# State steps of a gated delta rule: one product for two, smaller fill parts, another order on VectorE

## The chip, the cores and the metric

The kernel runs on one core of a Trainium2 chip. The metric is the device time of one execution in microseconds (us). The kernel is written instruction by instruction for each engine (TensorE or PE, VectorE or DVE, ScalarE or ACT, GpSimd or POOL, and SP, which issues the loads); the engines are kept in order by semaphores alone.

## The reference

Two layers of a decoder over 256 tokens of width 2048, all in float32:

```python
for l in range(DEPTH):                          # 2
    h = rms_norm(x, norm_mix_pre[l])
    p = h @ w_in[l]                             # columns shared out among three mixers
    mix = concat[gated_deltanet(6 heads), multiscale_pool(4 groups), swa_attention(6 heads)] @ w_out[l]
    x = x + rms_norm(mix, norm_mix_post[l])
    x = x + rms_norm(conv_glu_ffn(rms_norm(x, norm_ffn_pre[l])), norm_ffn_post[l])
```

The change lies in the delta rule. The 256 tokens are four chunks of 64 (C=64), a head is 128 wide, and after products within the chunks (an inverse, u, w, a_intra) a state S of 128x128 per head is carried over the chunks:

```python
def step(S, xs):
    u_n, w_n, q_n, k_n, a_n, c_n = xs
    v_new = u_n - w_n @ S
    o_n = q_n @ S + a_n @ v_new
    S = S * c_n + k_n.T @ v_new
    return S, o_n
```

Here q_n is q decayed within its chunk, and a_n is the attention within the chunk. The output o then goes through an RMS norm over the head and is multiplied by silu(z).

## The kernel before

**Large products.** A product with a weight matrix is made in fp32r as three: the weights are split into a high part (`w_hi`, ScalarE, L942) and the rest (`w_lo`, VectorE, L1159), so are the activations (`h_hi`, `h_lo`), and hi*hi, hi*lo and lo*hi are added up in PSUM (`three`, L1507). Weights come in pairs of column tiles, 2 MB each, into `raw` (two slots), issued by SP (L805), which waits until the `w_lo` parts of the pair two before are made. A pair has four parts of 1024 columns (four rows of k tiles), `hi_part` and `lo_part` make them, and TensorE uses a part in two halves (`half_a`, L1557), twelve records of 256 columns each; for `w_out` it is `out_half` (L1695), six records of 512 columns.

**Groups.** In the mixing stage the delta rule runs over three groups (NG) of two heads. TensorE's program for a group is `delta_pe` (L668). Wherever it would wait for VectorE or ScalarE it has fill: `more(count)` does the next `count` halves of the projection that later groups need (32 halves in each group). How many stand where is written out by hand in `FILL_FULL` (the first two groups, a loop) and `FILL_LAST` (the last group, whose fill is the pool projection's last part and the beginning of the output projection). VectorE's program is `delta_dve` (L493), ScalarE's `delta_act` (L362). Theirs have `more(place)` too: there it makes the low and high part number `place`, which TensorE uses some parts later.

**A state step.** A matrix of four [128,128] blocks m = 2h+t holds head h and token tile t; chunk c is half of such a tile. The four steps n have t = n // 2, c = n % 2. In a step TensorE waits for `state_ready`, makes w@S for both heads into bank 2 (L730), then q@S into bank 6 (L736), does one half of fill, waits for `v_new_ready`, makes the state's addition (L743) and adds a@v_new to bank 6 (L749). The stationary side of w and q has 64 columns, so these products are tiles of 128*64. VectorE makes v_new (L577) after w@S, and after L743 updates the state of both heads (L590), drains and releases the next step. Between these VectorE has a `w_lo` part (`more(11)`, after the first v_new) and the taps of the causal convolution for the next group's values (`taps`, L1391: three taps, two tiles each, every tap waits for the one before): taps 1 and 2 after the second v_new, tap 3 after the third. The convolution is begun by ScalarE (L1065).

**After the steps.** ScalarE squares o (L404) and copies it (L405), VectorE sums and scales it, GpSimd takes the root, VectorE normalizes (L604), TensorE turns it into bank 7, and VectorE multiplies by silu(z) (L608), which releases `delta_out`. Meanwhile TensorE does fill and turns the next group's q, k and v into banks 2 to 4 (or, in the last group, does the pool product, `pool_pe`).

An fp32 product is two records in the trace (two passes), an fp32r product one.

Of the kernel before, what the change touches and what calls it, by code (L numbers as in the profile page):

```python
# [98 lines left out]
                 states=(1, 1, 1, 1), out=2, end=0)  # L99
FILL_LAST = dict(turned=7, normed=2, products=2, n_turned=1, residual=(1, 1, 1, 1, 1), step=(1, 1, 1, 1, 1), uw=2,  # L100
                 states=(1, 1, 1, 1), out=2, end=2)
# [42 lines left out]
def trunk(nc, a, out):  # L144
    with ExitStack() as ctx:
# [60 lines left out]
        (q_s, k_s, v_s, z_s, qn, qd, kn, kbeg, kdec, vb, kn_t, qn_t, qd_t, e1, e2, vs, gb) = (  # L206
            scr[:, i, :] for i in range(17))
        pw, resid, inv, attn, u_m, w_t, o_m, low_m = q_s, k_s, v_s, qn, qd, kn, e1, e1
        v_new, state = vs[:, 0:256], vs[:, 256:512]

# [136 lines left out]
        def pool_act(act, l):  # L347
            act.wait_ge(sem("pool_mixed"), l + 1)
            for g in range(NPOOL):
                ins = act.activation(act_t[:, T_POOL + g, :], ps[:, 2 + g // 2, (g % 2) * T:(g % 2 + 1) * T],  # L350
                                     ACT.Copy, scale=par_all[:, l, R_PS + g:R_PS + g + 1])
# [10 lines left out]
        def delta_act(act, l, g, more, begin, ahead, last=False):  # L362
# [130 lines left out]
        def delta_dve(dve, l, g, more, finish, taps, windowed=lambda: None, second=3):  # L493
            v = l * NG + g + 1
            dve.drain()
# [77 lines left out]
            for n in range(4):  # L573
# [4 lines left out]
                                  ps[r, 2, 0:256].rearrange("p (h n) -> p h n", h=2),  # L578
                                  ALU.subtract).then_inc(sem("v_new_ready"), 1)
                if n == 0:  # L580
                    more(11)
                if n == 1:
                    taps(2, (1, 2))
                if n == 2:
                    taps(2, (3,))
                if n < 3:
                    dve.wait_ge(sem("state_add"), 3 * v - 2 + n)
                    for h in range(2):
                        sh = state[:, h * P:(h + 1) * P]
                        dve.scalar_tensor_tensor(sh, sh, gate_g[:, 5 + c, 2 * h + t:2 * h + t + 1],  # L590
                                                 ps[:, 3, h * P:(h + 1) * P], ALU.mult, ALU.add)
# [1264 lines left out]
```

## Time and profile before

| | us |
|---|---|
| median of 3 runs | 2325.9 |
| lowest and highest | 2325.8 and 2326.24 |
| the profiled execution | 2326.02 |
| its span, first to last instruction | 2324.2 |
| TensorE busy in it | 2305.2 (99%) |
| VectorE busy | 1617.7 (70%) |
| ScalarE busy | 1073.8 (46%) |

The granted clock of TensorE was 0.999 of its full speed. Busy time counts records, and those of TensorE overlap one another, since a product streams in while the one before drains; so a busy TensorE is not one at its peak, and what a piece of work costs on it is read from the starts of the records.

### The profile page before, as it was taken

How to read it: one execution, taken by the hardware profiler on the slowest of the kernel's cores; microseconds unless marked ns; L12 is line 12 of the kernel's file. 1: busy time of each engine (PE TensorE's matmuls, PEld its weight loads, DVE VectorE, ACT ScalarE, POOL GpSimd, SP SyncE). 2: the span in 40 equal slices, each digit the busy share in tenths (PEclk: the TensorE clock that was granted, in tenths of full speed). 3: DMA queues.
4: the chain of work that ended last, by engine and by line, in shares of the span. 5: the costliest groups of instructions: out<-in, count | busy, mean ns of one | idle time of the engine just before them, and what ended most of it. 6: DMA issues, size and time to landing. Idle time of an engine off the chain costs nothing.

```text
span 2324.2 us, 37134 instructions
## 1 busy us (share of the span) xinstructions
PE 2305.2 (99%) x13964; PEld 2041.7 (88%) x13964; DVE 1617.7 (70%) x2287; ACT 1073.8 (46%) x1398; POOL 39.5 (2%) x55
## 2 busy tenths in 40 slices
PE   9999999999999999999999999999999999999998
PEld 9999988888888888888899999888888888888887
DVE  5876665877787778555568676658778787785455
ACT  5454434644444444444455444346444444444443
POOL 0000010000000000000000000100000000000000
PEclk9999999999999999999999999999999999999999
DMA  7533326555665556555544433275655565555553
GB/s 243 170 121 109 124 94 204 177 180 183 196 195 185 180 187 215 194 182 203 199 146 146 137 102 124 74 235 168 193 181 180 193 195 190 180 201 207 188 185 141
DMA packets 295368, 401.29 MB, mean 173 GB/s; under 512 B 9320, under 2 KB 269570, under 8 KB 283522
## 3 DMA queue, kind: packets, MB, share of 16 engines
q1 hardware_dynamic: 294996, 400.19, 52.2%
q8 instruction: 49, 0.80, 0.1%
q10 hardware_dynamic: 302, 0.12, 0.0%
q14 instruction: 21, 0.17, 0.0%
HBM read 398.20 MB, written 2.10 MB: 172 GB/s over the span
## 4 chain that ended last, share of the span: by engine, by line
PE 94%; DVE 3%; DVEq 1%; ACT 1%; issue 1%; DMA 0%; ACTq 0%; SPq 0%; POOLq 0%; POOL 0%
PE ps L1528 28%; PE ps L1509 15%; PE ps L1510 15%; PE ps L1511 15%; PE ps L1534 14%; PE ps L673 2%; PE ps L678 1%; PE ps L730 1%; DVE w_lo L1159 1%; PE ps L743 1%; DVEq L1387 0%; ACT w_hi L942 0%; PE ps L736 0%; PE ps L1657 0%; DMA raw<-in_w_in 0%
## 5 line engine op out<-in xcount | busy, mean ns | idle before, releaser
L942 ACT ACTIVATE w_hi<-raw 128x1024 fp32r<-128x1024 f32 x740 | 779.7, 1059 | 984.1 <-PE ps L1534 522.1
L1159 DVE TENSOR_TENSOR w_lo<-raw,w_hi 128x1024 fp32r<-128x1024 f32 x744 | 895.8, 1224 | 465.4 <-ACT w_hi L942 457.5
L1528 PE MATMUL ps<-h_both,w_hi 128*128 128x512 f32 x2816 | 885.3, 396 | 1.2 <-DVE h_both L1181 1.2
L1534 PEld LDWEIGHTS ps<-h_both,w_lo 128*128 128x128 f32 x2816 | 529.0, 188 | 124.7
L1534 PE MATMUL ps<-h_both,w_lo 128*128 128x256 f32 x2816 | 553.9, 278 | 0.0
L1528 PEld LDWEIGHTS ps<-h_both,w_hi 128*128 128x128 f32 x2816 | 428.9, 189 | 1.9 <-issue 1.6
L1509 PE MATMUL ps<-w_hi,h_both 128*128 128x512 f32 x960 | 376.1, 392 | 0.9 <-DVE w_lo L1159 0.9
L1511 PE MATMUL ps<-w_hi,h_both 128*128 128x512 f32 x960 | 373.7, 389 | 0.0
L1510 PE MATMUL ps<-w_lo,h_both 128*128 128x512 f32 x960 | 373.7, 389 | 0.0
L1509 PE MATMUL ps<-h_both,w_hi 128*128 128x256 f32 x1216 | 354.7, 292 | 2.1 <-DVE h_both L1181 2.1
L1510 PE MATMUL ps<-h_both,w_hi 128*128 128x256 f32 x1216 | 343.8, 283 | 0.0
L1511 PE MATMUL ps<-h_both,w_lo 128*128 128x256 f32 x1216 | 343.7, 283 | 0.0
L1509 PEld LDWEIGHTS ps<-h_both,w_hi 128*128 128x128 f32 x1216 | 232.8, 191 | 6.0 <-issue 5.9
L1510 PEld LDWEIGHTS ps<-h_both,w_hi 128*128 128x128 f32 x1216 | 232.9, 192 | 0.1
L1511 PEld LDWEIGHTS ps<-h_both,w_lo 128*128 128x128 f32 x1216 | 232.6, 191 | 0.0
L1509 PEld LDWEIGHTS ps<-w_hi,h_both 128*128 128x128 f32 x960 | 180.2, 188 | 39.6 <-issue 2.9
L1511 PEld LDWEIGHTS ps<-w_hi,h_both 128*128 128x128 f32 x960 | 180.2, 188 | 37.7
L1510 PEld LDWEIGHTS ps<-w_lo,h_both 128*128 128x128 f32 x960 | 180.3, 188 | 36.4
L1471 DVE SCALAR_TENSOR_TENSOR scratch<-scratch,par 128x255 f32<-128x255 f32 (+1 forms) x352 | 154.6, 480 | 29.5 <-issue 28.9
L673 PE MATMUL ps<-scratch 128*128 128x128 f32 x672 | 86.9, 275 | 0.6 <-DVE scratch L555 0.6
L673 PEld LDWEIGHTS ps<-scratch 128*128 128x128 f32 x672 | 81.8, 191 | 2.5 <-DVE scratch L555 1.5
L1464 DVE TENSOR_SCALAR scratch<-scratch,par 128x256 f32<-128x256 f32 x176 | 64.7, 410 | 18.4 <-issue 18.1
(201 smaller groups left out, 1251.6 us busy)
## 6 DMA issues: line engine op xcount, KB each, us to landing
raw<-in_ffn_w_up SPq DMA_DIRECT2D x88, 2048.0 KB, 8.0
raw<-in_ffn_w_down SPq DMA_DIRECT2D x44, 2048.0 KB, 7.7
raw<-in_w_in SPq DMA_DIRECT2D x37, 2048.0 KB, 8.2
raw<-in_w_out SPq DMA_DIRECT2D x64, 512.0 KB, 6.4
x<-in_x SPq DMA_DIRECT2D x4, 512.0 KB, 7.0
raw<-in_w_in SPq DMA_DIRECT2D x4, 512.0 KB, 8.6
scratch<-in_norm_mix_post SPq DMA_DIRECT2D x2, 1024.0 KB, 9.5
scratch<-in_norm_ffn_post SPq DMA_DIRECT2D x2, 1024.0 KB, 10.0
```

The lines of the kernel that those rows point to most:

```text
L673: ins = pe.matmul(ps[:, bank, m * P:(m + 1) * P], w[:, m, :], r[:, m, :], start=True, stop=True)
L678: ins = pe.transpose(ps[:, bank, m * P:(m + 1) * P], mats(src)[:, m, :], ident)
L730: ins = pe.matmul(ps[r, 2, h * P:(h + 1) * P], w_t[:, cols], state[:, h * P:(h + 1) * P], start=True, stop=True)
L942: act.activation(w_hi[:, own(q, s), :], raw_part(l, q, s), ACT.Copy).then_inc(hi_done, 1)
L1159: dve.tensor_tensor(w_lo[:, own(q, s), :], raw_part(l, q, s), w_hi[:, own(q, s), :].bitcast(F32), ALU.subtract).then_inc(lo_done, 1)
L1464: dve.tensor_scalar(y_ab[:, ab, i, :], summed[:, ab, i, :], par_all[:, l, bass.ds(2 * j + (R_FC + 2 * 2 * FT + ab * FT + i), 1)], par_all[ ...
L1471: ins = dve.scalar_tensor_tensor(y, summed[:, ab, i, 0:T - k], par_all[:, l, bass.ds(2 * j + (R_FC + (2 - k) * 2 * FT + ab * FT + i), 1)], ...
L1509: pe.matmul(dst, w, xs, start=start, stop=False, skip_group_check=True)
L1510: pe.matmul(dst, w, xl, start=False, stop=False, skip_group_check=True)
L1511: return pe.matmul(dst, wl, xs, start=False, stop=True, skip_group_check=True)
L1528: pe.matmul(ps[:, up_bank(q - P_UP, i), :], w_hi[:, own(q, s), c:c + P], h_both[:, k, :, :].rearrange("p a n -> p (a n)"), start=k == 0, s ...
L1534: return pe.matmul(ps[:, up_bank(q - P_UP, i), 0:T], w_lo[:, own(q, s), c:c + P], h_hi[:, k, :], start=False, stop=True, skip_group_check= ...
```

## The change

Four edits in the state steps:

1. **Joint stationary side.** w and the decayed q are laid side by side in one buffer `wq` (for each block and chunk 64 columns of w beside 64 of q), and one product with 128 stationary columns gives w@S in one half of the rows of a bank and q@S in the other. For chunk 0 the bank is 6 with w in rows 0 to 63, for chunk 1 it is bank 2 with w in rows 64 to 127. The attention product adds to the half that holds q@S. The output so lies in two banks, by chunk, with its row halves exchanged, and is copied and squared in two pieces; the product with silu(z) undoes the exchange.
2. **Quarters.** Fill is done in quarters (one k tile of a part, six records of 256 columns, or one output tile, three of 512). A step has one quarter in the wait for v_new and one more after the attention product (`steps`); what is left over goes to `out`.
3. **Update by heads.** Each head's addition has a bank of its own (3 and 7) and a semaphore increment of its own, and TensorE waits for each head's state by itself.
4. **Taps.** In the groups that aren't last, tap 1 follows the first v_new, tap 2 the first update, tap 3 the second v_new; the `w_lo` part of place 11 follows the fourth v_new, and places 12 and 13 move back by one point each.

Before it turns the next group's q, k and v (or does the pool product, now in banks 3 and 6), TensorE waits for the output's copies.

```diff
-                 states=(1, 1, 1, 1), out=2, end=0)
+                 states=(0.5, 0.5, 0.5, 0.5), steps=(0.5, 0.5, 0.5), out=2.5, end=0)
...
+        wq = scr[:, 5:7, :].rearrange("p a (m n) -> p (a m) n", m=2).rearrange("p m (c n) -> p m c n", c=4)
+        w_of, qd_of = wq[:, :, 0:4:3, :], wq[:, :, 1:3, :]
+
+        def state_bank(c):
+            return 2 if c else 6
...
-            for i, dst in enumerate((kn_t, qn_t, qd_t)):
+            for i, dst in enumerate((kn_t, qn_t)):
                 act.wait_ge(sem("normed_turned"), 3 * v - 2 + i)
                 act.activation(dst, ps[:, 5 + i, :], ACT.Copy).then_inc(sem("normed_copied"), 1)
+            act.wait_ge(sem("normed_turned"), 3 * v)
+            act.activation(qd_of, ps[:, 7, :].rearrange("p (m c n) -> p m c n", m=4, c=2),
+                           ACT.Copy).then_inc(sem("normed_copied"), 1)
...
-            act.wait_ge(sem("o_done"), v)
-            act.activation(e2, ps[:, 6, :], ACT.Square).then_inc(sem("o_squared"), 1)
-            act.activation(o_m, ps[:, 6, :], ACT.Copy).then_inc(sem("o_copied"), 1)
+            for c in range(2):
+                act.wait_ge(sem("o_done"), 2 * v - 1 + c)
+                r = slice(CH * (1 - c), CH * (2 - c))
+                act.activation(e2[r, :], ps[r, state_bank(c), :], ACT.Square).then_inc(sem("o_squared"), 1)
+                act.activation(o_m[r, :], ps[r, state_bank(c), :], ACT.Copy).then_inc(sem("o_copied"), 1)
...
-            dve.tensor_copy(w_t, ps[:, 7, :])
+            dve.tensor_copy(w_of, ps[:, 7, :].rearrange("p (m c n) -> p m c n", m=4, c=2))
...
                 dve.tensor_tensor(v_new[r, :].rearrange("p (h n) -> p h n", h=2), mats(u_m)[r, t::2, :],
-                                  ps[r, 2, 0:256].rearrange("p (h n) -> p h n", h=2),
+                                  mats(ps[r, state_bank(c), :])[:, t::2, :],
                                   ALU.subtract).then_inc(sem("v_new_ready"), 1)
-                if n == 0:
+                if last and n == 0:
                     more(11)
-                if n == 1:
-                    taps(2, (1, 2))
-                if n == 2:
-                    taps(2, (3,))
+                if not last and n < 2:
+                    taps(2, (1 + 2 * n,))
+                if not last and n == 3:
+                    more(11)
                 if n < 3:
-                    dve.wait_ge(sem("state_add"), 3 * v - 2 + n)
                     for h in range(2):
+                        dve.wait_ge(sem("state_add"), 6 * v - 5 + 2 * n + h)
                         sh = state[:, h * P:(h + 1) * P]
                         dve.scalar_tensor_tensor(sh, sh, gate_g[:, 5 + c, 2 * h + t:2 * h + t + 1],
-                                                 ps[:, 3, h * P:(h + 1) * P], ALU.mult, ALU.add)
-                    dve.drain().then_inc(sem("state_ready"), 1)
+                                                 ps[:, 3 + 4 * h, 0:P], ALU.mult,
+                                                 ALU.add).then_inc(sem("state_ready"), 1)
+                    dve.drain()
+                    if not last and n == 0:
+                        taps(2, (2,))
...
-            more(13)
+            more(13 if last else 12)
...
-            more(14, 15)
+            more(*((14, 15) if last else (13, 14, 15)))
...
-                pe.wait_ge(sem("state_ready"), 4 * v - 3 + n)
                 for h in range(2):
                     m = 2 * h + t
-                    cols = slice(m * P + CH * c, m * P + CH * (c + 1))
-                    ins = pe.matmul(ps[r, 2, h * P:(h + 1) * P], w_t[:, cols], state[:, h * P:(h + 1) * P],
-                                    start=True, stop=True)
+                    pe.wait_ge(sem("state_ready"), 8 * v - 7 + 2 * n + h)
+                    ins = pe.matmul(ps[:, state_bank(c), m * P:(m + 1) * P],
+                                    wq[:, m, 2 * c:2 * c + 2, :].rearrange("p c n -> p (c n)"),
+                                    state[:, h * P:(h + 1) * P], start=h == 0, stop=False, skip_group_check=True)
                 ins.then_inc(sem("ws_done"), 1)
-                for h in range(2):
-                    m = 2 * h + t
-                    cols = slice(m * P + CH * c, m * P + CH * (c + 1))
-                    pe.matmul(ps[r, 6, m * P:(m + 1) * P], qd_t[:, cols], state[:, h * P:(h + 1) * P],
-                              start=h == 0, stop=False, skip_group_check=True)
                 more(fill["states"][n])
                 hold(pe, sem("v_new_ready"), 4 * v - 3 + n)
                 if n < 3:
                     for h in range(2):
                         m = 2 * h + t
-                        ins = pe.matmul(ps[:, 3, h * P:(h + 1) * P], kdec[r, m * P:(m + 1) * P],
-                                        v_new[r, h * P:(h + 1) * P], start=True, stop=True)
-                    ins.then_inc(sem("state_add"), 1)
+                        pe.matmul(ps[:, 3 + 4 * h, 0:P], kdec[r, m * P:(m + 1) * P], v_new[r, h * P:(h + 1) * P],
+                                  start=True, stop=True).then_inc(sem("state_add"), 1)
                 for h in range(2):
...
-                    ins = pe.matmul(ps[r, 6, m * P:(m + 1) * P], attn[r, cols], v_new[r, h * P:(h + 1) * P],
-                                    start=False, stop=True, skip_group_check=True)
-                if n == 3:
+                    ins = pe.matmul(ps[CH * (1 - c):CH * (2 - c), state_bank(c), m * P:(m + 1) * P], attn[r, cols],
+                                    v_new[r, h * P:(h + 1) * P], start=False, stop=True, skip_group_check=True)
+                if n >= 2:
                     ins.then_inc(sem("o_done"), 1)
+                if n < 3:
+                    more(fill["steps"][n])
             more(fill["out"])
+            pe.wait_ge(sem("o_copied"), 2 * v)
...
-            def half_a(l, q, j, n, s, half):
-                if half == 0:
+            def quarter_a(l, q, j, n, s, kk):
+                if kk == 0:
...
-                for kk in (2 * half, 2 * half + 1):
-                    ins = both_tiles(q, s, kk)
-                if half == 1:
+                ins = both_tiles(q, s, kk)
+                if kk == 3:
                     ins.then_inc(sub_used, 1)
```

## Rows read from the trace of the kernel before

**Rows 1.** The page: engines' busy time, and the chain that ended last.
```profile
PE 2305.2 (99%) x13964; PEld 2041.7 (88%) x13964; DVE 1617.7 (70%) x2287; ACT 1073.8 (46%) x1398; POOL 39.5 (2%) x55
...
PE 94%; DVE 3%; DVEq 1%; ACT 1%; issue 1%; DMA 0%; ACTq 0%; SPq 0%; POOLq 0%; POOL 0%
```
**Rows 2.** Timeline, TensorE, 194.3 to 200.4: start, duration, engine, line, operation, out<-in.
```profile
195.17 0.65 PE L730 MATMUL ps<-scratch 128*64 128x128 f32 x4 [0.15 <-DVEq L592]
...
196.18 0.39 PE L1509 MATMUL ps<-h_both,w_hi 128*128 128x256 f32 x1
196.41 0.28 PE L1510 MATMUL ps<-h_both,w_hi 128*128 128x256 f32 x1
...
197.59 0.28 PE L1511 MATMUL ps<-h_both,w_lo 128*128 128x256 f32 x1
197.80 0.71 PE L743 MATMUL ps<-scratch 64*128 64x128 f32 x4
198.44 0.65 PE L749 MATMUL ps<-scratch 64*64 64x128 f32 x4
199.24 0.65 PE L730 MATMUL ps<-scratch 128*64 128x128 f32 x4
```
**Rows 3.** Timeline, TensorE, last group of the first layer.
```profile
343.39 0.65 PE L730 MATMUL ps<-scratch 128*64 128x128 f32 x4
...
347.43 0.65 PE L730 MATMUL ps<-scratch 128*64 128x128 f32 x4
```
**Rows 4.** Timeline, TensorE, 186.2 to 188.3: the inverse's last products.
```profile
186.22 0.28 PE L1511 MATMUL ps<-h_both,w_lo 128*128 128x256 f32 x1
...
186.33 1.95 PE L673 MATMUL ps<-scratch 128*128 128x128 f32 x16
...
188.04 0.36 PE L1509 MATMUL ps<-h_both,w_hi 128*128 128x256 f32 x1
...
188.24 0.28 PE L1510 MATMUL ps<-h_both,w_hi 128*128 128x256 f32 x1
```
**Rows 5.** Timeline, TensorE, entry to the first step and exit of the fourth.
```profile
190.87 0.28 PE L1511 MATMUL ps<-h_both,w_lo 128*128 128x256 f32 x1
...
191.08 0.65 PE L730 MATMUL ps<-scratch 128*64 128x128 f32 x4
...
205.95 0.65 PE L749 MATMUL ps<-scratch 64*64 64x128 f32 x4
...
206.53 0.39 PE L1509 MATMUL ps<-h_both,w_hi 128*128 128x256 f32 x1
...
209.51 1.91 PE L678 MATMUL ps<-const,scratch 128*128 128x128 f32 x16
```
**Rows 6.** Timeline of VectorE and ScalarE; one line's durations; the page's w_lo row.
```profile
191.77 0.41 DVE L577 TENSOR_TENSOR scratch<-scratch,ps 64x256 f32<-64x256 f32 x1
...
192.23 0.90 ACT L1065 ACTIVATE act_t<-scaled,par 128x256 f32 x2
...
197.40 0.88 DVE L1391 SCALAR_TENSOR_TENSOR act_t<-scaled,par,act_t 128x254 f32 x2 [0.21 <-issue]
...
198.55 0.60 DVE L590 SCALAR_TENSOR_TENSOR scratch<-scratch,gate_g,ps 128x128 f32<-128x128 f32 x2 [0.27 <-PE ps L743]
...
L590 DVE SCALAR_TENSOR_TENSOR scratch<-scratch,gate_g,ps x36: 339/344/348, 194.5 to 1501.2; 128x128 f32<-128x128 f32 x36
...
L1159 DVE TENSOR_TENSOR w_lo<-raw,w_hi 128x1024 fp32r<-128x1024 f32 x744 | 895.8, 1224 | 465.4 <-ACT w_hi L942 457.5
```
**Rows 7.** Timeline, SP; DMA issues in 185 to 230, last column landing time.
```profile
193.48 19.55 SPq L805 DMA_DIRECT2D raw<-in_w_in  x2
...
raw<-in_w_in SPq DMA_DIRECT2D x2, 2048.0 KB, 8.1
```
**Rows 8.** Timeline, start of the second group.
```profile
216.15 2.12 ACT L942 ACTIVATE w_hi<-raw 128x1024 fp32r<-128x1024 f32 x2
...
222.77 1.47 PE L678 MATMUL ps<-const,scratch 128*128 128x128 f32 x12
```

More of the change, by code:

```diff
@@ L98 @@
 FILL_FULL = dict(turned=8, normed=2, products=2, n_turned=1, residual=(1, 1, 1, 1, 1), step=(1, 1, 1, 1, 2), uw=2,
-                 states=(1, 1, 1, 1), out=2, end=0)
+                 states=(0.5, 0.5, 0.5, 0.5), steps=(0.5, 0.5, 0.5), out=2.5, end=0)
 FILL_LAST = dict(turned=7, normed=2, products=2, n_turned=1, residual=(1, 1, 1, 1, 1), step=(1, 1, 1, 1, 1), uw=2,
-                 states=(1, 1, 1, 1), out=2, end=2)
+                 states=(0.5, 0.5, 0.5, 0.5), steps=(0.5, 0.5, 0.5), out=2.5, end=2)
 FEW_LATER = {0: 0, 1: 1, 3: 2, 4: 3, 5: 4, 7: 5, 8: 6, 9: 7, 10: 8, 11: 9, 12: 10, 14: 11, 15: 12}
@@ L491, in swa_dve, with delta_dve @@
             finish(1)
-        def delta_dve(dve, l, g, more, finish, taps, windowed=lambda: None, second=3):
+        def delta_dve(dve, l, g, more, finish, taps, windowed=None, second=3):
             v = l * NG + g + 1
+            last = windowed is not None
             dve.drain()
@@ L565, in delta_dve @@
             dve.wait_ge(sem("uw_done"), v)
-            dve.tensor_copy(w_t, ps[:, 7, :])
+            dve.tensor_copy(w_of, ps[:, 7, :].rearrange("p (m c n) -> p m c n", m=4, c=2))
             dve.memset(state, 0.0)
-            dve.drain().then_inc(sem("state_ready"), 1)
+            dve.drain().then_inc(sem("state_ready"), 2)
             finish(2)
@@ L1520, in part_a @@
                 if q < P_UP:
-                    for half in range(2):
-                        half_a(l, q, j, n, s, half)
+                    for kk in range(4):
+                        quarter_a(l, q, j, n, s, kk)
                 else:
@@ L1693, in out_tile, with out_quarter @@
                              w_hi[:, s, cols], w_lo[:, s, cols], xp == 0 and k == 0)
-            def out_half(l, u, k):
+            def out_quarter(l, u, k, t):
                 q, s, kind, xp = out_sub(u)
-                if k == 0:
+                if k == 0 and t == 0:
                     if u == 0:
@@ L1702, in out_half @@
                     pe.wait_ge(lo_done, l * SUBS + (4 * q + s + 9))
-                for t in range(TT):
-                    ins = out_tile(l, u, t, k, int(kind[1]), k)
-                if k == 1:
+                ins = out_tile(l, u, t, k, int(kind[1]), k)
+                if k == 1 and t == 1:
                     ins.then_inc(sub_used, 1)
@@ L1713, in out_rest @@
                         for k in range(2):
-                            out_half(l, u, k)
+                            for t in range(TT):
+                                out_quarter(l, u, k, t)
                         continue
@@ L1794, in more_of @@
                 def more_of(q, j, halves):
-                    left = iter(range(halves))
+                    left = iter(range(2 * halves))
                     def more(count):
-                        for n in itertools.islice(left, count):
-                            half_a(l, q + n // 8, j, q + n // 8, n // 2 % 4, n % 2)
+                        for n in itertools.islice(left, int(2 * count)):
+                            quarter_a(l, q + n // 16, j, q + n // 16, n // 4 % 4, n % 4)
                     return more
@@ L1807, in more_last @@
                 def more_last():
-                    left = iter(range(16 + 2 * N_SOON))
+                    left = iter(range(32 + 4 * N_SOON))
                     def more(count):
-                        for n in itertools.islice(left, count):
-                            if n < 16:
-                                half_a(l, P_POOL + n // 8, 0, P_POOL + n // 8, n // 2 % 4, n % 2)
+                        for n in itertools.islice(left, int(2 * count)):
+                            if n < 32:
+                                quarter_a(l, P_POOL + n // 16, 0, P_POOL + n // 16, n // 4 % 4, n % 4)
                             else:
-                                out_half(l, (n - 16) // 2, n % 2)
+                                out_quarter(l, (n - 32) // 4, n // 2 % 2, n % 2)
                     return more
```

25 lines of the change are left out of this document (14 added, 11 removed).

## The prediction

> **What bounds the kernel now.** I read the page first. TensorE is busy for 99% of the span and carries 94% of the chain that ended last, VectorE 3% [rows 1]. A change pays only if it takes time out of TensorE's own stream: fewer passes, cheaper switches between kinds of work, or less idling at its waits. VectorE, ScalarE and the loads matter only where they come late for it.
>
> Then I read TensorE's timeline through the state steps (two layers, three groups, four steps: 24 steps), since only they change what TensorE computes. In these rows an fp32 product is two records ("x4" is two products) and durations overlap, so I work with differences of starts. One cycle of the middle steps [rows 2]: the w product starts at 195.17, the q product follows, the fill (twelve fp32r records, a half part) at 196.18, the state product at 197.80, the attention product at 198.44, the next w product at 199.24. That is 4.07 us: 1.01 for w and q, 1.62 for the fill, 0.64 and 0.80 for the last two. The last 0.80 holds four passes, some 0.43, so 0.37 is idle until VectorE's update and drain are through. In the last group, whose fill has 512 columns, the cycle is 4.04 [rows 3].
>
> **Prices from the rows.** Fill records start 0.12 apart (196.41 to 197.59, ten steps) [rows 2]. Around a product of full 128*128 tiles the switch is cheap: last fill to first pass 0.11, sixteen passes in 1.71, so 0.107 each, and the first fill record then takes 0.20 to the next, 0.08 extra [rows 4]. Around half tiles (128*64, 64*128, 64*64) it is dearer: fill to w product 0.21 at 190.87 [rows 5], fill to state product 0.21, state to attention 0.64 for four passes, w and q 1.01 for eight, first fill record 0.23 [rows 2]; attention to fill 0.58 [rows 5].
>
> **The joint product (w and q in one stationary side).** Eight passes of 128*64 become four of 128*128. The trace has no such product between fills but for the inverse's, which is the same form and type, so I take its prices: 0.43 for four passes, no gap ahead, 0.20 for the first fill record. From w product to fill it is 0.43 instead of 1.01. It could cost up to twice that if loading 128 columns were what sets a pass (another 0.43 per step); the 0.107 per pass at 128 columns [rows 4] against 0.126 at 64 (1.01 over eight) speaks against it. The page "TensorE: Matmul & The Clock Gate" of the Trainium skill, section on LDWEIGHTS, says that a weight load takes time by its columns and not by its rows; by that rule four loads of 128 columns cost as much as eight of 64, and the joint product would save nothing. The trace disagrees: passes with 128 columns stand no further apart than those with 64, so the load is hidden here.
>
> **The quarter parts in both waits.** Fill work is only moved: six records ahead of the v_new wait instead of twelve, six between attention and the next w product. The second visit replaces the 0.37 of idling but brings a switch from a 64*64 tile to the fill, which the idle time now covers. Cycle after: joint product 0.43; six fill records 0.20+4x0.12+0.21=0.89; state product to attention 0.64; attention to fill 0.58; six fill records 0.23+4x0.12+0.11=0.82. Sum 3.36 against 4.07, 0.71 saved, in 18 cycles 12.8 us. In the last group a quarter is three records of 512 columns, about as long; same saving.
>
> **Ends of the chain of steps.** Ahead of the first step the gap of 0.21 becomes 0.11 or 0.12: 0.09 saved. The fourth step before: 2.63 from w to attention (as in the cycle), 0.58 to the fill, 2.98 of 24 records to the turns [rows 5]: 6.19. After: 0.43+0.89+0.58, then 30 records in 2.98+0.72: 5.60; 0.59 saved. Both six times: 4.1 us. Without stalls the change gives 12.8+4.1=16.9 us.
>
> **Does v_new arrive in time?** With less fill ahead of the wait, the margin shrinks. VectorE starts v_new 0.69 after the w product and takes 0.41 [rows 6]; with at most 0.09 to release TensorE (the update ends at 198.55+0.60, the w product starts at 199.24, a drain included [rows 2, 6]) it is ready at 1.19, the state product can start at 1.32. It is hidden by 0.13 as long as VectorE is free. The two state updates take 0.60 together, one alone 0.34 [rows 6]; by heads, the first can start some 0.5 after the state product starts, and TensorE wants the first state 2.04 after it. Hidden too, by about a microsecond.
>
> **The taps one by one.** This is where I see a cost. In the four groups that are not last, VectorE's program now has after the first v_new: tap 1 (waits until ScalarE has begun the convolution), updates, a drain, tap 2, second v_new. ScalarE's beginning ends at 192.23+0.90=193.13 [rows 6], hardly movable, as it follows the part released by the last fill ahead of the steps. The old program hid this behind a w_lo part. New: joint product at 190.99; v_new 191.7 to 192.2; tap 1 from 193.2 to 194.1 (0.88 a pair); update of head 0 until 194.45, of head 1 until 194.70. TensorE wants head 0 at 190.99+3.36=194.35 and gets it at 194.5: 0.15 lost. Then a drain (0.21, the idle time in [rows 6]) and some more for the second drain in a row, tap 2 from 195.0 to 195.9, and only then the second v_new, which could have started at 194.5+0.69=195.2: it is ready at 196.4 instead of by 195.8, 0.58 lost. The third tap follows it (0.21+0.88, to 197.5), the update ends near 198.1, TensorE wants it at 198.4: hidden. So 0.73 is lost per such group, 2.9 us in four. The last group has no taps; its w_lo part after the first v_new (1.22 [rows 6]) ends before the update is wanted.
>
> **The w_lo part moved behind the fourth v_new.** Its reader is the second quarter after the last attention product: the part is done 0.69+0.41+1.22=2.3 after the fourth joint product, wanted at 1.90+0.82=2.7: hidden by 0.4, and without that cover up to 1 us a group. SP's queue waits for this part before it issues the raw load of the pair after next. It went out at 193.48 and takes 8.1 to land [rows 7]; now, with the fourth joint product at 198.44+3.36=201.8, at about 204.2, landing at 212.3, while ScalarE first reads it near 215 (216.15 before [rows 8]; my estimate is 1 earlier now, half of what TensorE has gained by then). Hidden by 2.7; nothing is queued in SP behind it but later raw loads. The output's Square and Copy come in two row halves (twice the instructions on ScalarE, the first pair during the fourth step), TensorE's new wait for the copies before the turns has the 3.7 of 30 fill records ahead of it, the product with z in two pieces adds about 0.2 to VectorE ahead of the next group, whose turn at 222.77 [rows 8] had over 1 us to spare. The copies into strided places (w, q): same size and engine, I take no cost; if VectorE's doubled, v_new would be 0.65 late six times, 3.9 us. The attention product now goes from one row half to the other column half, the same 64*64 form: no cost taken, at most one more gap of 0.21 per step, 5.0 us.
>
> **Sum.** 16.9-2.9=14.0 us. The profiled execution took 2326.02 (span 2324.2), the median of the runs is 2325.9; so 2312.0.
>
> **Rivals.**
> - **No stall (2309).** If a tap pair and the updates overlap more than I drew, or drains in a row cost nothing, the whole 16.9 stays. Against it: ScalarE's end at 193.13 is fixed. 0.15.
> - **More waiting than drawn (2316 to 2318).** v_new's margin of 0.13 turns into a wait of 0.1 to 0.2 in all 24 steps, or the crossed tile costs its gap: 2 to 5 us less. For it: the thin margin. 0.18.
> - **The joint product costs twice (2322).** 24x0.43=10.3 us of the gain is gone, 3.7 remain, no change to be told. By the rule on weight loads this is the outcome, and the rows above speak against it. 0.04.
> - **The late raw load (slower, 2333).** If it lands later than about 12 us after its issue, ScalarE's first part of the next group, VectorE's w_lo behind it and then the normed operands are late, and TensorE stops at its turns. The gain is gone where each of the four groups loses 3.5; with 5.2 lost in each the time is 2333. In the profile the queue is otherwise empty there, so 0.03.
> - **Forecast (2310 to 2314).** 0.60.
>
> **How the numbers follow.** The likeliest is 2312. The range takes in the first two rivals and the bounds of the crossed tile and the strided copy: 2308 to 2318. A measurement of this kernel tells 0.2% (4.7 us) from no change. Forecast, no stall and more waiting are all faster: 0.93; the double price is "same", 0.04; the load is slower, 0.03.
>
> **What would show it.** In the profile after: the q product's line gone, four-record joint products of 128*128 with the fill 0.43 behind; w-product starts 3.4 apart in the last group and at the third cycle elsewhere, 3.5 and 3.9 in the first two cycles of the other groups; TensorE waiting on the second v_new there, with VectorE in tap 2; raw loads issued 10 us later with no wait on them. If cycles are 3.8 everywhere, a switch is mis-sized; if TensorE waits at v_new in the last group too, the margin was; if ScalarE waits for raw w_in, it is the load.

## The result, and the profile after

The changed kernel takes 2311.97 us (median of 4 runs, 2311.82 to 2312.16) against 2326.07 for the kernel before, measured beside it: ratio 0.9939, 95% interval 0.9922 to 0.9956. That is 14.1 us less; 14.0 was forecast (2312.0).

The page of the changed kernel, busy times and the chain that ended last:

```profile
PE 2291.5 (99%) x13868; PEld 2032.9 (88%) x13868; DVE 1618.6 (70%) x2293; ACT 1079.5 (47%) x1410; POOL 39.6 (2%) x55
...
PE 92%; DVE 3%; DVEq 1%; ACT 1%; issue 1%; DMA 0%; POOL 0%; ACTq 0%; SPq 0%; POOLq 0%
```

Against [rows 1], TensorE has 96 records fewer (13964 to 13868): the four passes of the q product in 24 steps. Its busy time falls by 13.7 us, the span by 13.8.

TensorE, VectorE, ScalarE and SP through the steps of the first group (lines have moved: the joint product is L747, the state product L756, attention L761, v_new L588, the update L601, the taps L1406, fill L1524):

```profile
191.02 0.60 PE L747 MATMUL ps<-scratch 128*128 128x128 f32 x4
...
191.38 0.37 PE L1524 MATMUL ps<-h_both,w_hi 128*128 128x256 f32 x1
...
191.66 0.41 DVE L588 TENSOR_TENSOR scratch<-scratch,ps 64x256 f32<-64x256 f32 x1
...
192.26 0.89 ACT L1080 ACTIVATE act_t<-scaled,par 128x256 f32 x2
...
192.27 0.71 PE L756 MATMUL ps<-scratch 64*128 64x128 f32 x4
...
192.91 0.65 PE L761 MATMUL ps<-scratch 64*64 64x128 f32 x4
193.42 0.88 DVE L1406 SCALAR_TENSOR_TENSOR act_t<-scaled,par,act_t 128x255 f32 x2 [1.35 <-ACT act_t L1080]
...
193.49 0.38 PE L1524 MATMUL ps<-h_both,w_hi 128*128 128x256 f32 x1
...
194.22 0.60 DVE L601 SCALAR_TENSOR_TENSOR scratch<-scratch,gate_g,ps 128x128 f32<-128x128 f32 x2
...
194.62 0.75 PE L747 MATMUL ps<-scratch 128*128 128x128 f32 x4 [0.15 <-DVE scratch L601]
...
195.11 0.88 DVE L1406 SCALAR_TENSOR_TENSOR act_t<-scaled,par,act_t 128x254 f32 x2 [0.30 <-issue]
...
196.00 0.42 DVE L588 TENSOR_TENSOR scratch<-scratch,ps 64x256 f32<-64x256 f32 x1
...
196.57 0.68 PE L756 MATMUL ps<-scratch 64*128 64x128 f32 x4 [0.50 <-DVE scratch L588]
...
198.58 0.60 PE L747 MATMUL ps<-scratch 128*128 128x128 f32 x4
...
201.86 0.61 PE L747 MATMUL ps<-scratch 128*128 128x128 f32 x4
...
204.35 0.37 SPq L820 DMA_DIRECT2D raw<-in_w_in  x1
```

The joint product runs on into the fill after 0.36 (191.02 to 191.38) where [rows 2] had 1.01. Joint products start at 191.02, 194.62, 198.58 and 201.86: cycles of 3.60, 3.96 and 3.28, 10.84 together; forecast 3.51, 3.94 and 3.36, 10.81. VectorE's first tap waits for ScalarE (192.26+0.89) and starts at 193.42; the update follows only at 194.22 and the joint product at 194.62; tap 2, at 195.11, holds back the second v_new to 196.00, and TensorE waits for it until 196.57. SP issues the raw load at 204.35. In the last group, which has no taps, the cycle is 3.25 against 4.04 in [rows 3]:

```profile
334.27 0.61 PE L747 MATMUL ps<-scratch 128*128 128x128 f32 x4
...
337.52 0.61 PE L747 MATMUL ps<-scratch 128*128 128x128 f32 x4
...
348.61 0.47 PE L1524 MATMUL ps<-w_hi,h_both 128*128 128x512 f32 x1 [0.18 <-DVE w_lo L1174]
```

TensorE's waits for VectorE in the steps (total us, times, longest), the first being the second v_new in each of the four groups:

```profile
PE ps L756 <- DVE scratch L588: 2.0, 4, 0.5
...
PE ps L747 <- DVE scratch L601: 0.3, 2, 0.2
```

### The profile page after: what moved, and what is told of

Its sections match the earlier page's. It is cut to its first block, busy times and chain, and to the rows that moved or that the text cites. A ratio compares the mean times of both kernels' runs of the same rounds, so it can differ in the third digit from the quotient of the medians.

```text
span 2310.4 us, 37016 instructions
## 1 busy us (share of the span) xinstructions
PE 2291.5 (99%) x13868; PEld 2032.9 (88%) x13868; DVE 1618.6 (70%) x2293; ACT 1079.5 (47%) x1410; POOL 39.6 (2%) x55
## 4 chain that ended last, share of the span: by engine, by line
PE 92%; DVE 3%; DVEq 1%; ACT 1%; issue 1%; DMA 0%; POOL 0%; ACTq 0%; SPq 0%; POOLq 0%
PE ps L1543 28%; PE ps L1524 15%; PE ps L1526 14%; PE ps L1525 14%; PE ps L1549 14%; PE ps L691 2%; PE ps L696 1%; DVE w_lo L1174 1%; DVEq L1402 1%; ACT w_hi L957 0%; PE ps L761 0%; PE ps L756 0%; PE ps L1671 0%; DVE act_t L1406 0%; PE ps L747 0%
## 5 line engine op out<-in xcount | busy, mean ns | idle before, releaser
L1524 PE MATMUL ps<-w_hi,h_both 128*128 128x512 f32 x960 | 376.6, 392 | 1.2 <-DVE w_lo L1174 1.2
L1524 PE MATMUL ps<-h_both,w_hi 128*128 128x256 f32 x1216 | 355.7, 292 | 2.0 <-DVE h_both L1196 2.0
L1524 PEld LDWEIGHTS ps<-h_both,w_hi 128*128 128x128 f32 x1216 | 232.8, 191 | 5.2 <-issue 5.0
L1524 PEld LDWEIGHTS ps<-w_hi,h_both 128*128 128x128 f32 x960 | 180.2, 188 | 39.7 <-issue 3.3
```

What stands on the lines that cost most here:

```text
L1524: pe.matmul(dst, w, xs, start=start, stop=False, skip_group_check=True)
```

## The experiments

All are edits of the changed kernel, timed beside the kernel before, which took 2325.96 to 2326.12 in these comparisons (medians). Differences of under 0.5 us are not read as effects. The interval of a ratio is 2 to 3 us wide to either side. The differences of 2 to 4 us between two experiments therefore rest on medians of four or more runs, which lie within 0.8 us of one another for each kernel, and on the cycles in the traces, which repeat from one group to the next of its kind within 0.03.

### 1. VectorE's order as before

```diff
-                if last and n == 0:
+                if n == 0:
                     more(11)
-                if not last and n < 2:
-                    taps(2, (1 + 2 * n,))
-                if not last and n == 3:
-                    more(11)
+                if not last and n == 1:
+                    taps(2, (1, 2))
+                if not last and n == 2:
+                    taps(2, (3,))
```

The `w_lo` parts of places 12 and 13 also go back to where they were (not shown).

> The changed kernel with VectorE's order of the kernel before: the w_lo part of place 11 after the first v_new, taps 1 and 2 after the second, tap 3 after the third. Theory A (the order of taps costs two stalls of TensorE in each of four groups, 1.06 us a group in the profile of the changed kernel): the first cycle falls from 3.60 to 3.25 us, TensorE's wait on the second v_new (2.0 us in all) is gone; taps 1 and 2 together (1.97 us) make the second update late by some 0.2 us. Gain over the changed kernel 0.8x4=3.2 us: about 2308.8. Rival B (taps one by one are what makes the steps short; in the old order the second update is late by the second tap's length): slower by 0.9x4, about 2315.

Measured: 2309.39 us, ratio 0.9928 (0.9915 to 0.9942), 2.6 less than the changed kernel. TensorE's wait on the second v_new is gone. The joint products start at 190.84, 194.12, 197.62 and 201.04: cycles of 3.28, 3.50 and 3.42, so the two taps together do make the second update late by some 0.2, and tap 3 the third by 0.14. The new order of the taps, one edit of the change, loses.

### 2. An order that stands in no wait

```diff
-                if last and n == 0:
+                if n == 0:
                     more(11)
-                if not last and n < 2:
-                    taps(2, (1 + 2 * n,))
-                if not last and n == 3:
-                    more(11)
+                if not last and n > 0 and n < 3:
+                    taps(2, (2 * n - 1,))
...
-                    if not last and n == 0:
+                    if not last and n == 1:
                         taps(2, (2,))
```

The `w_lo` parts of places 12 and 13 also go back to where they were.

> The changed kernel with quarters, and VectorE's order such that no piece stands in a wait: the w_lo part of place 11 after the first v_new, tap 1 after the second v_new, tap 2 after the second update, tap 3 after the third v_new. Theory A: all cycles are 3.25 to 3.3 us in all groups, no wait of TensorE on v_new or state: 1.06x4 = 4.2 us faster than the changed kernel, 2307.7. Rival B (the stalls in the four groups come from somewhere else than the taps, such as ScalarE's beginning of the convolution or two banks read at a time): same as the changed kernel, 2311 to 2312.

Measured: 2308.05 us, ratio 0.9922 (0.9909 to 0.9936), 3.9 less than the changed kernel. TensorE and VectorE in the first group:

```profile
192.26 0.71 PE L754 MATMUL ps<-scratch 64*128 64x128 f32 x4
...
193.12 0.59 DVE L599 SCALAR_TENSOR_TENSOR scratch<-scratch,gate_g,ps 128x128 f32<-128x128 f32 x2
...
194.29 0.61 PE L745 MATMUL ps<-scratch 128*128 128x128 f32 x4
...
194.94 0.42 DVE L588 TENSOR_TENSOR scratch<-scratch,ps 64x256 f32<-64x256 f32 x1 [1.22 <-PE ps L745]
...
195.39 0.88 DVE L1404 SCALAR_TENSOR_TENSOR act_t<-scaled,par,act_t 128x255 f32 x2
...
196.29 0.61 DVE L599 SCALAR_TENSOR_TENSOR scratch<-scratch,gate_g,ps 128x128 f32<-128x128 f32 x2
...
197.19 0.88 DVE L1404 SCALAR_TENSOR_TENSOR act_t<-scaled,par,act_t 128x254 f32 x2 [0.30 <-issue]
...
197.57 0.61 PE L745 MATMUL ps<-scratch 128*128 128x128 f32 x4
```

The update at 193.12 comes behind a `w_lo` part instead of a tap that waits for ScalarE, tap 1 (195.39) and tap 2 (197.19) lie in the open stretches, and both cycles are 3.28.

### 3. Half parts, no fill after the attention product

```diff
-                 states=(0.5, 0.5, 0.5, 0.5), steps=(0.5, 0.5, 0.5), out=2.5, end=0)
+                 states=(1, 1, 1, 1), steps=(0, 0, 0), out=2, end=0)
```

(and the same in `FILL_LAST`)

> The changed kernel with half parts in the wait for v_new and no fill after the attention product (states 1, steps 0, out 2), the joint product, the update by heads and the order of taps kept. Theory A (after the update by heads the state is ready before the attention product is through, so the second visit of fill covers nothing and costs its switches, 0.58+0.23+0.11 for six records against about 0.1): a cycle without stall of 3.14 instead of 3.25 us in the last group; in the others the wider wait for v_new takes the stall on the second v_new away: about 10.1 for three cycles instead of 10.84. 0.7x4+0.3x2 = 3.7 us faster than the changed kernel: 2308.3. Rival B (the quarter after the attention product covers an idle time of 0.37 as in the kernel before): a cycle of 3.4 to 3.5, 18x0.2 = 3 to 4 us slower, 2315 to 2316.

Measured: 2309.99 us, ratio 0.9931 (0.9917 to 0.9944), 2.0 less than the changed kernel, between the two theories. In the last group my 3.14 holds for the first cycle alone (330.00 to 333.14), whose joint product comes behind fill. The second and third are 3.25 and 3.23; here are the joint products of the second, with the state product between them:

```profile
333.14 0.71 PE L747 MATMUL ps<-scratch 128*128 128x128 f32 x4
...
335.18 0.71 PE L756 MATMUL ps<-scratch 64*128 64x128 f32 x4
...
336.39 0.71 PE L747 MATMUL ps<-scratch 128*128 128x128 f32 x4
```

The cycle is 3.25, as with quarters. The attention product is followed after 0.58 by whatever comes, joint product or fill, and the first passes behind it cost 0.11 more: the second visit of fill neither saves nor costs. Nearly all of the 2.0 us comes from the other four groups, where twelve records of fill ahead of the v_new wait take in tap 2 (second cycle 3.35 instead of 3.96); the stall in the first cycle, 3.60, is still there.

### 4. Two products in opposite column halves

```diff
-                    ins = pe.matmul(ps[:, state_bank(c), m * P:(m + 1) * P],
-                                    wq[:, m, 2 * c:2 * c + 2, :].rearrange("p c n -> p (c n)"),
-                                    state[:, h * P:(h + 1) * P], start=h == 0, stop=False, skip_group_check=True)
+                    ins = pe.matmul(ps[r, state_bank(c), m * P:(m + 1) * P], wq[:, m, 3 * c, :],
+                                    state[:, h * P:(h + 1) * P], start=h == 0, stop=False, skip_group_check=True)
...
+                    pe.matmul(ps[CH * (1 - c):CH * (2 - c), state_bank(c), m * P:(m + 1) * P], wq[:, m, 1 + c, :],
+                              state[:, h * P:(h + 1) * P], start=h == 0, stop=False, skip_group_check=True)
```

> The changed kernel with the joint product undone: from the same buffer a product of 64 columns for w and then one for q, into the same halves of the banks. Theory A: from w product to fill it is 1.01 us again instead of 0.36, 0.65 more per step, less the stalls of 1.06 us a group that this covers in four groups: (2.6-1.06)x4+2.6x2=11.4 us, about 2323.4. Rival B (the gain came from the quarters, the update by heads and the covered idle time; the joint product pays in loads of 128 columns what it saves in passes): under 4 us slower, at most 2316.

Measured: 2316.82 us, ratio 0.996 (0.9947 to 0.9974): 4.9 more than the changed kernel, far from 11.4 and just beyond the rival's 4. TensorE at the first step (L747 is w, L752 is q, fill L1527, state product L759):

```profile
190.89 0.32 PE L747 MATMUL ps<-scratch 128*64 128x128 f32 x1
190.90 0.32 PE L752 MATMUL ps<-scratch 128*64 128x128 f32 x1
191.05 0.27 PE L747 MATMUL ps<-scratch 128*64 128x128 f32 x1
191.06 0.27 PE L752 MATMUL ps<-scratch 128*64 128x128 f32 x1
...
191.48 0.39 PE L1527 MATMUL ps<-h_both,w_hi 128*128 128x256 f32 x1
...
192.38 0.71 PE L759 MATMUL ps<-scratch 64*128 64x128 f32 x4
```

The records of w and q start 0.01 apart: products in opposite halves of the columns run side by side. From w to fill it is 0.59, not 1.01. So this kernel undid less than it was meant to, and a proper control had to keep both in the same half. In the last group, where nothing stalls, its cycle is 3.60 against 3.25. In the other groups the cycles are 3.61, 3.94 and 3.61: the longer step covers the first stall of the changed kernel whole and the second in part, which is why 0.35 a cycle shows up as no more than 4.9 us. (The Trainium skill says under "TensorEngine Tiling (Array Packing)", Key Properties, that different tiles can load and multiply in parallel; these rows agree.)

### 5. Two products in the same column half

The w product goes to bank 2 and the q product to bank 6, both in rows `r`, as before the change; all else stays changed.

```diff
+                    ins = pe.matmul(ps[r, 2, h * P:(h + 1) * P], wq[:, m, 3 * c, :],
+                                    state[:, h * P:(h + 1) * P], start=True, stop=True)
...
+                    pe.matmul(ps[r, 6, m * P:(m + 1) * P], wq[:, m, 1 + c, :], state[:, h * P:(h + 1) * P],
+                              start=h == 0, stop=False, skip_group_check=True)
```

> The changed kernel with the joint product undone as in the kernel before: w product into bank 2, q product into bank 6, both in the same half of the columns, the rest (quarters, update by heads, order of taps, pieces of the output's copies) as changed. The kernel with two products in opposite halves ran them side by side and lost only 4.9 us. Theory A (products in the same column half run one after the other, and what the joint product saves over the kernel before is 0.65 a step): 1.01 from w product to fill, the stalls of 1.06 a group covered in four groups: 11.4 us slower than the changed kernel, 2323.4. Rival B (the halves don't matter, two products of 64 columns cost the same wherever they go): 2316.8.

Measured: 2325.39 us, ratio 0.9998 (0.9989 to 1.0007): no change from the kernel before, 13.4 more than the changed kernel. A cycle of TensorE (w at 195.01, q, fill, state product, attention, fill, next w):

```profile
195.01 0.65 PE L747 MATMUL ps<-scratch 128*64 128x128 f32 x4
...
195.50 0.60 PE L752 MATMUL ps<-scratch 128*64 128x128 f32 x4
...
196.03 0.39 PE L1527 MATMUL ps<-h_both,w_hi 128*128 128x256 f32 x1
...
196.93 0.71 PE L759 MATMUL ps<-scratch 64*128 64x128 f32 x4
...
197.57 0.65 PE L764 MATMUL ps<-scratch 64*64 64x128 f32 x4
...
198.15 0.39 PE L1527 MATMUL ps<-h_both,w_hi 128*128 128x256 f32 x1
...
199.05 0.65 PE L747 MATMUL ps<-scratch 128*64 128x128 f32 x4
```

It is 4.04, with 0.49 and 0.53 for the two products, one after the other. TensorE doesn't idle any more, but the cycle is hardly shorter than the 4.07 of [rows 2]: the idle time has become two switches, attention to fill and fill to a 128*64 tile. My 11.4 had left out that the gap of 0.21 ahead of the w product comes back as well, 0.1 in 24 steps, 2.4 us; with it the sum is 13.8.

Experiments 4 and 5 differ in the banks too: in 4 both products go to one bank, in 5 to two. The rows speak for the halves as the cause: w's own two products (the x4 at 195.01) and those of experiment 4 go to one half of one bank, and their passes start 0.11 apart, like those of w and q in the same half. Opposite halves in different banks were not run.

### 6. The joint product alone

Half parts as in 3, VectorE's order as in 1, and the update of both heads together:

```diff
-                    for h in range(2):
-                        dve.wait_ge(sem("state_add"), 6 * v - 5 + 2 * n + h)
+                    dve.wait_ge(sem("state_add"), 6 * v - 4 + 2 * n)
+                    for h in range(2):
...
-                                                 ps[:, 3 + 4 * h, 0:P], ALU.mult,
-                                                 ALU.add).then_inc(sem("state_ready"), 1)
-                    dve.drain()
+                                                 ps[:, 3 + 4 * h, 0:P], ALU.mult, ALU.add)
+                    dve.drain().then_inc(sem("state_ready"), 2)
```

> Of the changed kernel the joint product alone (with its two banks, the output's pieces and the wait for the copies): half parts in the wait, no fill after the attention product, both heads updated after both state products with one release, VectorE's order as in the kernel before. Theory A (the joint product by itself brings nearly all; the kernel with everything but the joint product ran in 2325.4): as the kernel with half parts, order without stalls and common update, 2312.2, and 0.3 more in each of four groups, where taps 1 and 2 (1.97) end after the second state product: 2313.4. Rival B (the edits need each other: alone the joint product brings less than half): 2319 or more.

Measured: 2313.64 us, ratio 0.9947 (0.9933 to 0.996). Against the 2326.12 measured beside it that is 12.5 us less: of the 14.1 us of the whole change, 12.5 come from the joint product alone, and the other three edits together add 1.6. The cycle in the last group is 3.48, with a wait for VectorE's update that the other edits take away; the expected 2313.4 was close.

### 7 to 9. Half parts or quarters, update by heads or together

All three have the joint product and the order of experiment 2. The first has half parts and the update by heads, the second half parts and the common update, the third quarters and the common update.

> Half parts in the wait for v_new, no fill after the attention product, update by heads, joint product, and the order on VectorE that has no stall (w_lo part after the first v_new, taps at the second v_new, the second update and the third v_new). Theory A (with the update by heads the state comes in time either way; the trace of the kernel with half parts shows 3.25 us in the last group, the same as with quarters): 2308.0, as with quarters in this order. Rival B (quarters gain by covering the wait): 0.1 to 0.3 a cycle slower, 2310 to 2313.

> As the kernel with half parts and the order without stalls, but both heads updated after both state products, then a drain and one release, as before the change. Theory A (now nothing covers the update: released 0.75+0.60+0.09=1.44 after the state product starts, wanted at 1.22): each of 18 cycles 0.2 to 0.25 longer, 3.25 to 3.5: 4 us slower, 2312. Rival B (update by heads gives nothing of its own): 2308.

> Quarters, joint product, order without stalls, but both heads updated after both state products with a drain and one release. Theory A (the update by heads is worth something only where no fill stands after the attention product; the quarter there covers 0.8): 2308.1, no change from the update by heads; with half parts the same edit cost 4.0. Rival B (the release by heads gains on its own): 2310 to 2312.

Measured, with experiment 2 as the fourth corner:

| | update by heads | common update |
|---|---|---|
| quarters | 2308.05 | 2308.25 |
| half parts | 2308.11 | 2312.16 |

The ratios are 0.9923 (0.991 to 0.9937) for half parts by heads, 0.9941 (0.9927 to 0.9954) for half parts with the common update, 0.9923 (0.991 to 0.9937) for quarters with the common update. In the last group of half parts with the common update, the joint product again waits for the state:

```profile
333.38 0.71 PE L744 MATMUL ps<-scratch 128*128 128x128 f32 x4 [0.15 <-DVEq L601]
...
335.43 0.71 PE L753 MATMUL ps<-scratch 64*128 64x128 f32 x4
...
336.07 0.65 PE L758 MATMUL ps<-scratch 64*64 64x128 f32 x4
...
336.87 0.71 PE L744 MATMUL ps<-scratch 128*128 128x128 f32 x4
```

From attention to joint product (336.07 to 336.87) it is 0.80 instead of 0.58, and the cycle (333.38 to 336.87) 3.49 instead of 3.25: 0.22 in 18 cycles is 4.0 us. Quarters and update by heads are two ways to the same 4 us; the second to be made adds nothing.

### 10 and 11. A wide attention product

In the kernel of experiment 2 the attention block is stored with its column halves exchanged, and the product takes all 128 columns (the other chunk's half of the block is zero):

```diff
+                    for c in range(2):
+                        ins = dve.tensor_tensor(a4[:, :, 1 - c, :], p4[:, :, c, :], d4[:, :, c, :], ALU.mult)
...
-                    ins = pe.matmul(ps[CH * (1 - c):CH * (2 - c), state_bank(c), m * P:(m + 1) * P], attn[r, cols],
+                    ins = pe.matmul(ps[:, state_bank(c), m * P:(m + 1) * P], attn[r, m * P:(m + 1) * P],
```

> Quarters and the order without stalls; besides, the attention product takes the whole block of 128 stationary columns: the block is zero outside its chunk, and it is stored with its column halves exchanged (two VectorE instructions instead of one), so the other half of the rows gets zeros added and the result is the same. Its tile becomes 64*128, as the state product's. Theory A (the 0.64 from state to attention product are four passes and a gap of 0.21 for the change of tile form): 0.43 instead of 0.64 in 18 steps, 3.8 us faster than with the narrow tile: 2304.2. Rival B (every product with 64 rows has such a gap, or the wider column load costs it back): no change, 2308.

Measured: 2307.09 us, ratio 0.9919 (0.9905 to 0.9932), 1.0 less than experiment 2. In the last group:

```profile
334.66 0.60 PE L748 MATMUL ps<-scratch 128*128 128x128 f32 x4
...
335.90 0.71 PE L757 MATMUL ps<-scratch 64*128 64x128 f32 x4
...
336.45 0.61 PE L761 MATMUL ps<-scratch 64*128 64x128 f32 x4
...
337.79 0.60 PE L748 MATMUL ps<-scratch 128*128 128x128 f32 x4
```

State to attention product is now 0.55 (was 0.64), and the cycle 3.13 (was 3.25). The change of tile form costs some 0.1 there, not the 0.21 that I read out of 0.64; a second gap, at the entry into 64-row tiles, stays. Of the 2.2 us that 18 cycles would give, 1.0 arrives. A group takes 70.22 from first joint product to first joint product, against 70.44, so 0.2 less where the three cycles alone are shorter by 0.4. Of what is missing, 0.06 lies in the fourth step, which has no state product: there the attention product itself enters the 64-row tiles, and it takes 0.64 to the fill (201.70 to 202.34) instead of 0.58. Another 0.07 is lost in the inverse, where TensorE waits 0.23 for VectorE instead of 0.16; the rest stays open.

> Half parts, order without stalls, update by heads, and the attention product with 128 stationary columns. Theory A (quarters and halves cost TensorE the same as long as the state comes in time; from state product to next joint product there are now some 1.1, the first head is released after 0.92, the second after 1.2, wanted at 1.3): as with quarters, 2307.1. Rival B (the shorter attention product uncovers the update): 18x0.1 to 0.2 slower, 2309 to 2310.5.

Measured: 2306.73 us, ratio 0.9917 (0.9903 to 0.9931): the fastest here, 19.4 us under the kernel before and 5.2 under the changed one. It is 0.4 under the same with quarters, which I don't read as an effect.

## Why the prediction was right

**The bound.** TensorE carried the chain, and what its stream lost the kernel lost: 13.7 us of busy time, 14.1 of time.

**The joint product** was priced by the inverse's full-tile products, at 0.43 to the fill; it is 0.36. The 0.107 a pass was 1.71 over sixteen, an average that hides how the products end. The last three passes and the fill behind them:

```profile
187.78 0.50 PE L673 MATMUL ps<-scratch 128*128 128x128 f32 x3
188.04 0.36 PE L1509 MATMUL ps<-h_both,w_hi 128*128 128x256 f32 x1
```

From the first of the three to the fill it is 0.26: passes start 0.112 apart, and the fill starts only 0.03 behind the last. Four passes so take 3x0.112+0.03, which is the 0.36 measured; 0.07 a cycle was to be had from these rows beforehand. The 0.126 for 64 columns was an average too, with the switches on both sides in it: within the eight passes of [rows 2] the trace has 0.109. So columns hardly set how far apart passes start (0.109 and 0.112). The conclusion of the prediction stands, the comparison of 0.107 with 0.126 that it leaned on doesn't.

The double price is refuted by experiment 5: with eight loads of 64 columns in place of four of 128 the time is 13.4 us worse, not equal. That doesn't refute the rule of the Trainium skill ("TensorE: Matmul & The Clock Gate", LDWEIGHTS) that a load's time goes by its columns. It is about the load itself, and the load records of w before and of the joint product after (shortest, median and longest in ns) agree with it in direction:

```profile
L730 PEld LDWEIGHTS ps<-scratch x96: 132/137/137, 191.1 to 1501.9; 128*64 128x64 f32 x96
L747 PEld LDWEIGHTS ps<-scratch x96: 186/190/193, 190.9 to 1488.2; 128*128 128x128 f32 x96
```

Loads with half the rows and 128 columns (the state product, L756) take 0.187. They don't prove the rule: the loads of the turns (L696) have 128 columns and take 0.14. A load of 0.190 stands beside passes 0.11 apart, so the loads overlap. What fails is the step from the price of a load to the price of a pass.

My account of where the saving lies was incomplete: from 2325.39 (same half) to 2316.82 (opposite halves) 8.6 us were to be had without a joint stationary side, and the last 4.9 need one load. The stalls blur that split. In the last groups, which have none, the cycles are 4.02, 3.60 and 3.25: 0.42 for the opposite halves and 0.35 for the joint side.

**The quarters** were credited with covering the idle 0.37, as a part of 0.71 a cycle. The cycle without stall came out at 3.25 in the last groups and 3.28 in the others (experiment 2), against 3.36. The 0.37 was too large: with no wait the next work starts 0.58 behind the attention product and not 0.43 (experiment 3), so of the 0.80 only 0.22 could be won. The cover is real, and no gain of their own: with two narrow products it brings nothing (experiment 5), with the update by heads nothing (3, 7), with the common update 4 us (8, 9). The prediction had these edits in one sum and didn't say that either would have done.

**v_new** arrived in time wherever VectorE was free: in the last groups no wait is listed. The rival with a wait in every step fell, but more narrowly than the reckoned margin of 0.13 says. The 0.09 from VectorE's end to TensorE was read from the update. For v_new it is 0.15, as the second step shows, where TensorE does wait (196.00+0.42 to 196.57). Where nothing stalls the state product starts 0.16 to 0.20 behind v_new, so the margin was 0.02 to 0.05, and in the last groups' first step, at 0.15, there was none. That nothing was lost here is in part luck.

**The taps** were the cost: named in place and mechanism, mis-sized. 2.9 us were forecast, from cycles of 3.51 and 3.94 against 3.36. Against the 3.28 of experiment 2, which has these groups without stalls, the stalls are 0.32 and 0.68, 4.0 us in four groups; taking the order away gave 3.9. The first tap started 0.27 after ScalarE's end where I had allowed 0.07, and the unstalled cycle was shorter than I thought. The larger gain (0.08 in twelve cycles, 0.11 in six, 1.6 us) and the larger loss (1.1 us) pull against each other.

**The sum.** That 14.1 stands beside 14.0 is luck: its three terms are off by 1.6 (cycle), 1.1 (taps) and 0.6 us (ends), not all the same way. Over the span of 13.8 the three cycles of the six groups save 10.3 (12.24 to 10.84 in four, 12.12 to 9.77 in two), where 12.8-2.9=9.9 was forecast, and all the rest 3.5, where the ends were to give 4.1. The ends give some 0.7 in a group that isn't last, as forecast, and only some 0.3 in the last.

**The moved `w_lo` part and the raw load.** Issued at 204.35 (forecast 204.2), with 8.2 us to land (the median of these loads), so near 212.6, and first read by ScalarE at 214.58 (forecast 215): hidden by 2. The next group's turn stands at 220.66, 2.1 earlier than in [rows 8]. In the last group the fill behind the output's turn waits 0.18 for its `w_lo` part (348.61, above), a loss that I had not written down and a part of what the last group's end lacks.

**The crossed tile and the strided copies** cost nothing to be seen: attention to fill is 0.58 as in [rows 5], VectorE's copy of w takes 0.686 where it took 0.684, and v_new starts 0.64 after the joint product.

## What to carry to other kernels

Read a price from single starts, the last one and the switch behind it included; an average over a run of passes had the joint product wrong by a fifth. Before crediting several edits with one idle time, ask which of them alone would close it: here the edit that shortens the stream brought 12.5 us, two others close the same gap of 4 us, and the fourth gave 2.6 to 3.9 of it back. An instruction that waits for a third engine doesn't belong between a product and the update that its engine owes TensorE, however short it is. A part of the work that fills a wait must be charged with its switches, and two half-width products should lie in opposite column halves where they can't be made one.

## What the runs showed of the hardware

Two products of 128*64 with the same moving operand in opposite column halves start 0.01 us apart; eight passes and the way to the fill take 0.59, in the same half 1.01, as one product of 128 columns 0.36. An edit meant as a plain undoing thus left more than half of the gain in place. Passes of 64 columns in one half start 0.109 apart, passes of 128 columns 0.112, and a full-tile product is followed by fill 0.03 after its last pass, a 128*64 product only after 0.20. A change between 64*128 and 64*64 tiles costs about 0.1 in all, and from attention product to what follows it is 0.58 for four passes, fill or joint product alike (0.54 with 64*128 tiles). From the end of a VectorE instruction to TensorE it is 0.06 for the state (194.56 to 194.62, the first head's update) and 0.15 for v_new.
